# Sliding attention in one inference step: the rotary half swap on VectorE, softmax's small operations per pair of heads, and another order of pairs

## The reference, cut to what matters

```
q, k, v = split(rms_norm(x) @ w_qkv)        # 16 query heads, 4 key/value heads, 64 wide
q, k = rope(q), rope(k)                     # [x1*cos - x2*sin, x2*cos + x1*sin], halves of 32
s = q @ k^T / 8, masked by chunks of 64 (own chunk and two before)
m = max(max(s), sink); p = exp(s - m)
p = p / (sum(p) + exp(sink - m))
out = (p @ v) @ w_out
```

## Time and profile before

| | |
|---|---|
| runs, us | 1117.15, 1115.31, 1117.17 |
| profiled execution, us | 1115.43 |
| its span, us | 1113.6 |
| TensorE busy | 1103.8 us (99%) |
| VectorE busy | 703.9 us (63%) |
| ScalarE busy | 511.2 us (46%) |
| GpSimd busy | 114.1 us (10%) |
| mean granted TensorE clock | 0.995 |

### The profile page before, as it was taken

The page is one execution under the profiler, slowest core; times in us unless marked ns, Lnnn a source line. Parts: engine busy times, 40 slices in busy tenths (PEclk is TensorE's granted clock), DMA queues, the critical chain, the costliest instruction groups (busy, mean ns, idle before and its releaser), DMA issues.

```text
span 1113.6 us, 21313 instructions
## 1 busy us (share of the span) xinstructions
PE 1103.8 (99%) x8147; PEld 1080.8 (97%) x8147; DVE 703.9 (63%) x1079; ACT 511.2 (46%) x760; POOL 114.1 (10%) x146
## 2 busy tenths in 40 slices
PE   9999999999999999999999999999999999999998
PEld 8999999998999999999999999999988899999998
DVE  7766665474665876665546666655599776666442
ACT  6544443363554544444335444433466554444331
POOL 0000001200002600000210000011142410000011
PEclk9999999999999999999999999999999999999999
DMA  7544454333233644445434445543332244444431
GB/s 274 190 151 173 179 183 178 118 114 109 100 129 111 207 172 167 172 165 206 159 113 168 172 151 173 201 164 142 114 148 92 83 173 160 172 167 179 176 136 43
DMA packets 24493, 172.07 MB, mean 155 GB/s; under 512 B 3280, under 2 KB 3568, under 8 KB 5888
## 3 DMA queue, kind: packets, MB, share of 16 engines
q1 hardware_dynamic: 22320, 167.45, 42.0%
q0 software_dynamic: 960, 2.23, 0.6%
q10 hardware_dynamic: 1168, 1.77, 0.5%
HBM read 168.88 MB, written 2.56 MB: 154 GB/s over the span
## 4 chain that ended last, share of the span: by engine, by line
PE 93%; DVE 4%; ACT 1%; DMA 1%; issue 1%; POOL 0%; SPq 0%; DVEq 0%; ACTq 0%
PE acc L395 30%; PE acc L397 29%; PE acc L396 29%; DVE wlo L382 1%; DMA raw<-in_w 1%; PE num L464 1%; DVE rstd L1042 1%; PE mb L675 0%; PE mb L694 0%; PE mb L609 0%; PE num L601 0%; PE acc L722 0%; ACT work L955 0%; ACT whi L353 0%; PE mb L422 0%
## 5 line engine op out<-in xcount | busy, mean ns | idle before, releaser
L395 PE MATMUL acc<-xhi,whi 128*128 128x288 f32 x1680 | 502.2, 299 | 0.3 <-DVE wlo L382 0.3
L353 ACT ACTIVATE whi<-raw 128x1024 fp32r<-128x1024 f32 (+1 forms) x290 | 326.6, 1128 | 381.2 <-PE acc L397 363.3
L396 PE MATMUL acc<-xlo,whi 128*128 128x288 f32 x1680 | 497.0, 296 | 0.0
L397 PE MATMUL acc<-xhi,wlo 128*128 128x288 f32 x1680 | 495.3, 295 | 0.0
L382 DVE TENSOR_TENSOR wlo<-raw,whi 128x1024 fp32r<-128x1024 f32 (+1 forms) x290 | 384.2, 1326 | 158.0 <-ACT whi L353 147.3
L395 PEld LDWEIGHTS acc<-xhi,whi 128*128 128x128 f32 x1680 | 316.1, 188 | 3.0 <-issue 1.8
L397 PEld LDWEIGHTS acc<-xhi,wlo 128*128 128x128 f32 x1680 | 317.7, 189 | 0.0
L396 PEld LDWEIGHTS acc<-xlo,whi 128*128 128x128 f32 x1680 | 316.8, 189 | 0.5
L395 PE MATMUL acc<-ahi,whi 128*128 128x288 f32 x832 | 247.1, 297 | 0.9 <-DVE alo L1279 0.7
L396 PE MATMUL acc<-alo,whi 128*128 128x288 f32 x832 | 245.4, 295 | 0.0
L397 PE MATMUL acc<-ahi,wlo 128*128 128x288 f32 x832 | 244.6, 294 | 0.0
(11 more groups left out here) (225 smaller groups left out, 642.9 us busy)
## 6 DMA issues: line engine op xcount, KB each, us to landing
raw<-in_w SPq DMA_DIRECT2D x113, 1024.0 KB, 4.8
raw<-in_w SPq DMA_DIRECT2D x32, 1408.0 KB, 5.8
x<-in_xT SPq DMA_DIRECT2D x4, 288.0 KB, 5.3
raw<-in_w SPq DMA_DIRECT2D x4, 256.0 KB, 4.8
out_yT<-x ACTq DMA_DIRECT2D x2, 288.0 KB, 2.2
out_yT<-x SPq DMA_DIRECT2D x2, 288.0 KB, 2.3
work<-in_cst POOLq DMA_DIRECT2D x1, 560.0 KB, 4.2
work<-in_c ACTq DMA_DIRECT2D x1, 514.0 KB
```

Source lines behind the costliest of these rows:

```text
L353: act.activation(dst, src, ACT.Copy).then_inc(hi_done, 1)
L395: pe.matmul(out, wh, hi[:, k, :], start=(first and n == 0), stop=False)
L396: pe.matmul(out, wh, lo[:, k, :], start=False, stop=False)
L397: mm = pe.matmul(out, wl, hi[:, k, :], start=False, stop=(last and n == len(tiles) - 1))
```

## The change

- The permutation matmul goes. The channels of each q and k head are laid out in another order on the host (`ROPE_DIM`, undone for the key output), so that partners are 16 partitions apart within a block of 32. VectorE's `stream_shuffle` then swaps them while it reads the piece from PSUM, a second operation multiplies the piece by the cosine, and GpSimd multiplies the shuffled one by the sine and adds. The reciprocal of the norm and the tables are made ahead of the first evacuation. The stage has 16 groups in PSUM instead of 24.
- The negated maximum, the denominator's sum and the reciprocal are made once for the two heads of a pair. A new small sum (`s_z`) lets ScalarE make the sink's exponential once per pair. One of a pair's four scalings goes to ScalarE (`scaled`).
- The order of pieces has q1 ahead of v0. Pairs start at the pieces of `PAIR_AT`, from the third on; the sample's second pair comes before the last prompt pair. An odd tick stands between the two halves of a piece. A set of transposes comes three ticks behind its item instead of two. `FILL` holds 84 matmuls instead of 48.
- The transposed v is copied in two groups (`turn`, `last`).

```diff
-SWA_PIECES = ["k0", "q0", "v0", "q1", "q2", "q3", "k1", "q4", "q5", "q6", "v1", "q7"]
+SWA_PIECES = ["k0", "q0", "q1", "v0", "q2", "q3", "k1", "q4", "q5", "q6", "v1", "q7"]
-TURN_AFTER = {"q1": "v0", "v1": "v1"}
+TURN_AFTER = {"q2": "v0", "v1": "v1"}
-FIRST_TICK = 4
+PAIRS = [("p", 0), ("p", 1), ("p", 2), ("p", 3), ("s", 0), ("p", 4), ("p", 5), ("p", 6), ("s", 1), ("p", 7)]
+NP = len(PAIRS)
+PAIR_AT = {2: 0, 3: 1, 5: 2, 6: 3, 7: 4, 8: 5, 9: 6, 10: 7}
+TAIL_TICKS = range(2 * len(PAIR_AT), 2 * NP + 5)
+FILL = {17: [(0, [0, 1])], 18: [(0, [2, 3])], 19: [(1, [0, 1]), (1, [2, 3]), (2, [0, 1])], 20: [(2, [2, 3])],
+        21: [(3, [0, 1]), (3, [2, 3])], 23: [(0, [4, 5, 6])], 24: [(m, [4, 5, 6]) for m in (1, 2, 3)]}
...
+ROPE_DIM = np.array([16 * (l // 32) + l % 16 + 32 * (l % 32 // 16) for l in range(HD)])
+SWAP_16 = [i ^ 16 for i in range(32)]
```

TensorE (the bodies of `transposes`, `pair_scores` and `values` are those of the old tick, cut apart; `transposes` also waits for ScalarE's scaling):

```diff
             def tick(t, G0):
+                transposes(t - 3)
+                if t % 2 == 0:
+                    pair_scores(t // 2)        # waits: neg_ready of the pair before, rope_done or ks_ready
+                else:
+                    values((t - 5) // 2, G0)   # waits: pt_ready, evac of ("last", v), olo_ready
...
             def swa_in(i):
                     if what == "piece":
                         if n == 0:
                             first_two(i, c0_, G0)
                         if n > 1:
-                            in_piece(i, 0, c0_ + n, g, G0 + g)
-                    elif what == "swap":
-                        pe.wait_ge(evac, max(G0 + group_of("piece", p) + 1, G0 + g - 3))
-                        pe.matmul(bank, perm, s_raw[:, ROPE.index(p) % 2, :], start=True, stop=True).then_inc(turn_mm, 1)
+                            t = 2 * PAIR_AT[n - 1] + 1 if n - 1 in PAIR_AT else None
+                            in_piece(i, 0, c0_ + n, g, G0 + g, between=None if t is None else lambda: tick(t, G0))
+                        if n in PAIR_AT:
+                            tick(2 * PAIR_AT[n], G0)
```

ScalarE:

```diff
+                probs_turned(t - 3)
+                if t % 2 == 0:
+                    scaled(t // 2 - 1)
+                    outputs_hi((t - 6) // 2)
+                    exps(t // 2)
...
+                for n, p in enumerate(SWA_PIECES):
+                    hi_ahead(0, c0_ + n)
+                    if n in PAIR_AT:
+                        tick(2 * PAIR_AT[n])
+                        tick(2 * PAIR_AT[n] + 1)
```

VectorE and GpSimd:

```diff
                     if what == "piece":
+                        if n == 0:
+                            rms(norm + 1)
+                            dve.tensor_tensor(rc, cos, rstd[:, :], ALU.mult)
+                            dve.tensor_scalar(nsnk, sinks, -1.0, None, ALU.mult)
+                            own(dve.tensor_tensor(rs, sin, rstd[:, :], ALU.mult))
...
+                            if xi >= 2:
+                                dve.wait_ge(rope_done, xi - 1)
+                            dve.stream_shuffle(s_sw[:, xi % 2, :], bank, SWAP_16)
+                            dve.tensor_tensor(s_t1[:, xi % 2, :], bank, rc, ALU.mult).then_inc(evac, 1)
+                        if n in PAIR_AT:
+                            outputs_lo(PAIR_AT[n] - 3)
+                            scores(PAIR_AT[n])
+                        lo_ahead(0, c0_ + n)
+                        if n in PAIR_AT:
+                            divide(PAIR_AT[n])
...
+                pool.tensor_tensor(s_sw[:, b, :], s_sw[:, b, :], rs, ALU.mult).then_inc(t1_ready, 1)
                 pool.wait_ge(t1_ready, xi + 1)
+                pool.tensor_tensor(dst, s_t1[:, b, :], s_sw[:, b, :], ALU.add).then_inc(rope_done, 1)
```

More of the change, by code:

```diff
@@ L644, in mlstm_out @@
                 mix_rest(i)
-            def tick(t, G0):
[L649 to L702, removed]
-                        for u in range(2):
-                            kv = 2 * c + u
-                            pe.matmul(mb[3][u * HD:(u + 1) * HD, 0:128], s_v[0:TS, 2, kv * HD:(kv + 1) * HD],
-                                      probT[0:TS, (t - 4 + u) % 4, 128:256], start=False, stop=True, **kw).then_inc(pv_mm, 1)
@@ new lines, in transposes @@
+            def transposes(n):
+                if not 0 <= n < 2 * NP:
+                    return
+                pe.wait_ge(p_ready, n + 1)
+                if PAIRS[n // 2][0] == "p":
+                    pe.wait_ge(p_act, sum(k == "p" for k, _ in PAIRS[:n // 2 + 1]))
+                if n >= 1:
+                    pe.wait_ge(pt_ready, n)
+                pr = prob[:, n % 4, :]
+                if PAIRS[n // 2][0] == "p":
+                    for j in range(3):
+                        mm = pe.transpose(mb[2][:, j * P:(j + 1) * P], pr[:, j * P:(j + 1) * P], ident)
+                else:
+                    pe.transpose(mb[2][:, 0:P], pr[:, 0:P], ident)
+                    mm = pe.transpose(mb[2][0:TS, P:2 * P], pr[:, P:P + TS], ident)
+                mm.then_inc(pt_mm, 1)
@@ new lines, in divide @@
+            def divide(n):
+                if not 0 <= n < NP:
+                    return
+                b = n % 2
+                p = PAIRS[n][0] == "p"
+                parts = ((0, P), (P, 3 * P)) if p else ((0, CACHE + TS),)
+                J = len(parts)
+                dve.wait_ge(exp_ready, n + 1)
+                own(dve.tensor_tensor(s_den[:, b, :, 0:J], s_sum[:, b, :, 0:J], s_sk[:, b, :, 0:J], ALU.add))
+                dve.reciprocal(s_inv[:, b, :, 0:J], s_den[:, b, :, 0:J]).then_inc(inv_ready, 1)
+                dve.wait_ge(inv_ready, n + 1)
+                for u in range(2):
@@ L1308, in swa_in @@
[L1308 to L1316 removed]
+                            xi = ROPE.index(p)
                             if xi >= 2:
@@ new lines, in swa_in @@
+                        if n in PAIR_AT:
[4 more added lines that the diff above has]
+                            divide(PAIR_AT[n])
+                    else:
+                        j = int(p[1]) * P
+                        bank = acc[(g + BANK) % 4]
+                        dve.wait_ge(turn_mm, TURNS.index((what, p)) + 1)
+                        if what == "turn":
@@ L1331, in swa_in @@
-                    tick(t)
+                        outputs_lo((t - 6) // 2)
+                        scores(t // 2)
+                        divide(t // 2)
             dve.memset(zero[:, :].bitcast(F32), 0.0).then_inc(z_ready, 1)
@@ L1453, in _ @@
             pool.dma_start(a["kT_out"], s_k[:, :, TP - P:T]).then_inc(out_dma, 16)
-            pool.wait_ge(evac, G0 + group_of("turn", "v1") + 1)
+            pool.wait_ge(evac, G0 + group_of("last", "v1") + 1)
             pool.dma_start(a["v_out"][0:P, :], s_v[:, 1, :]).then_inc(out_dma, 16)
@@ L1509, in layouts @@
     first = {"q": 0, "k": KD, "v": KD + 2}
-    a["w8"] = pieces(q[:, [first[p[0]] + int(p[1]) for p in SWA_PIECES]].reshape(D, -1), 2)
+    q = q[:, [first[p[0]] + int(p[1]) for p in SWA_PIECES]]
+    for n, p in enumerate(SWA_PIECES):
+        if p in ROPE:
+            q[:, n] = q[:, n].reshape(D, 2, HD)[:, :, ROPE_DIM].reshape(D, P)
+    a["w8"] = pieces(q.reshape(D, -1), 2)
     a["w9"] = pieces(pairs(v["swa_w_out"][0], 0), 2)
```

319 lines of the change are left out of this document (165 added, 154 removed).

## The result

The changed kernel took 1131.92 us (median of four runs, 1130.77 to 1132.86), beside 1116.23 us for the kernel before on the same chip (four runs, 1114.27 to 1117.17): ratio 1.0138, 95% interval 1.0117 to 1.0158. It is slower, by 15.7 us. The forecast was 1126.8 us in a range of 1120.5 to 1132.5: the sign and the range hold, 5 us of size are missing. The range holds narrowly: the median lies 0.6 us inside its upper end.

The account below looks back on a forecast made before the run. TensorE was taken as the bound nearly everywhere. The terms, 6.9 + 1.2 + 2.9 + 3.5 + 2.5 + 2.2 - 5.9 - 2.7 = +10.6 us, led to 1126.8 us, range 1120.5 to 1132.5.

Parts of the forecast that it names:

- First scores: TensorE stall after the third piece, waiting for k0 and q0 to be rotated: 6.9 us, bounds 5.0 and 7.0.
- The clock: TensorE's granted clock dropping after the idle time before the first scores: 1.2 us lost, bounds 0 and 3.
- Small stalls: Waits for q2's rotation, for VectorE and ScalarE between pieces, and before the first late fill: together 2.9 us.
- the ring: VectorE and ScalarE operations done in turn per piece: 6.2 to 6.3 us a round, stopping TensorE a little.
- Values of pair 4: In the middle of the last piece, values wait for turned v1's copy: 3.5 us, bounds 2.7 and 4.0.
- Sample pair: Its scores, after the last piece, wait for q7's rotation: stall 2.5 us, bounds 2.3 and 3.3.
- Old waits credited: TensorE's earlier waits, mostly in the tail, removed by more fill: 2.7 us saved, bounds 0 and 2.7.
- Swaps: Ten permutation matmuls of 0.59 us each leave TensorE: 5.9 us saved, bounds 5.0 and 7.2.
- halves: Cutting 8 pieces in two around transposes and values costs TensorE 0.27 us each: 2.2 us, bounds 0 and 3.
- The beat without waits: TensorE's time per pair of heads and piece: 6.3 us before, less 0.59, plus 0.27, gives 6.0 us.
- rival (b): 0.7 us more ring stalls in six pieces and a second slow clock stretch: +6, about 1133 us; chance 0.10.

Follow-up runs that it names:

- lock1: part1 with GpSimd's sine product and add cut to the last 32 columns, sine part left out elsewhere: 1116.50 us, ratio 1.0013.
- locka: The changed kernel with GpSimd's sine product and add cut to the last 32 columns: 1127.94 us, ratio 1.0111.
- warm: The changed kernel with 44, 22 and 18 unused products of zeros in TensorE's three long waits: 1127.22 us, ratio 1.0110.
- turn: The changed kernel with VectorE copying the turned v1 before the last piece's division, not after: 1127.62 us, ratio 1.0116.
- best1: The changed kernel with seven pairs from the fifth piece on, another fill and more last projection work in three tiles: 1121.14 us, ratio 1.0058.
- best3: best2 with 24 products of zeros before the first scores: 1119.87 us, ratio 1.0040.
- part1: The kernel before with the half swap on VectorE's shuffle; also adjacent ticks and turned v copied in two groups: 1121.55 us, ratio 1.0067.
- best2: The changed kernel with pairs from the fourth piece, first evacuations before splits, earlier v1 copy, moved fill, more last projection work: 1121.19 us, ratio 1.0066.

## Why the prediction was right, and where its size was off

**First scores (6.9 us).** 6.73 measured, released by GpSimd's add, whose two first steps fell against the splits as worked out (1.71 and 1.79). Right. My upper bound of 7.0 held; the lower, 5.0 if they shared, is excluded by lock1 and locka, where a 32-column step lasts as long as the split beside it.

**The clock (1.2 us).** This is the term that failed, and by more than its upper bound of 3. warm puts it at 5.4 us of stage. I counted one dip of 1.5 us and gave the second to a rival. From the first scores to the second pair's the changed kernel needs 6.19 us (810.21 to 816.40), warm 4.25: the first dip slowed TensorE by 1.9 us. From the last piece's values to the second set of values behind them, without what lies between the transposes and the sample pair's scores, it needs 14.98 us (862.86 to 881.09), warm 10.59 (859.50 to 873.66): the second dip slowed it by 4.4. The waits of 3.48 and 3.25 us lie only 5.4 us apart, and the clock was not back between them. Together that is 6.3 us of TensorE's own work. turn, which halves the first of these waits, gets back 1.7 us beyond its waits.

**Small stalls (2.9 us).** 0.7 at q2, 0.6, 0.2 and 0.3 for ScalarE's copies in the ring, 1.1 before the late fill: 2.9. Right in sum; q2's was half of what I took, the ring's a little more.

**Values of pair 4 (3.5 us).** 3.48; turn shows the cause.

**Sample pair (2.5 us).** 3.25, the upper bound: GpSimd's add fell beside the last piece's split (1.65 instead of 0.8). I knew the mechanism and left it out of the value.

**Old waits credited (2.7 us).** They went, but a new one came that I had not looked for: 1.36 us ahead of the projection's fifth tile (896.39), which waits for VectorE's low split. FILL takes 84 matmuls out of the first four tiles, so each has only three left at the end, and the split of the fifth tile's weights has no cover. best1 to best3 give three tiles more work there, and it is gone.

**Swaps (-5.9) and halves (+2.2).** No run isolates them. With the other terms as measured, and with TensorE's whole slowing since the waits are taken as the changed kernel has them, 6.73 + 6.3 + 2.9 + 3.48 + 3.25 + 1.36 - 2.7 = 21.3, against 17.2 of the stage, they come to -4.1, where I had -3.7. The beat without waits is 5.9, predicted 6.0.

The misses are then 5.1 (clock), 0.75 (sample), 1.36 (fifth tile), -0.4 (swaps and halves) and -0.2 (first scores): together 6.6 us, the difference between +10.6 and +17.2. That the median still fell inside the range is in part luck: its value is nearer to the 1133 of rival (b), which had the second slow stretch, than to my 1126.8. The other half of that rival, 0.7 us more of ring stalls in six pieces, did not come.

**What I left out.** That a copy and a multiply on VectorE become a shuffle and a multiply is true of the counts, but says nothing of what runs beside them. part1 shows that the swap on VectorE, put into the old order, costs 6.8 us of stage instead of saving 5.9. By lock1, 4.3 of that come from GpSimd's steps, which now follow the evacuation at once and meet VectorE's scaling and split; its share of the clock is in both numbers. How much part1 loses by its two ticks side by side is not shown. The changed order hides this in the steady pieces, where GpSimd takes 0.80 and 0.81; at both ends it doesn't.

**What stays open.** What decides whether the clock falls behind the tail's short waits (best2 and best3 differ there), and whether the pairwise operations alone, with the permutation matmul kept, would gain; that kernel was not run. Why best1 to best3 still lose, between ScalarE's copies, VectorE's chain and the clock, is read from their waits and not tested one by one.

## What to carry to other kernels

An operation taken off the busiest engine is only worth its time if what replaces it doesn't sit in front of the first consumer: count the chain from the input to the first use at both ends of the stage, not only the beat. When a change makes an engine idle for several microseconds, price the clock behind it too, and look at where the next wait stands: here two waits 5.4 us apart had one slow stretch of 13.7 us around them. And if work moves to GpSimd, look at which of VectorE's SBUF operations it will stand beside.

## What the runs showed of the hardware

- A shuffle of 128x288 from PSUM is recorded with 0.48 us and takes 0.37 to the next start (803.80 to 804.17), of which loading its mask is 0.01: my 0.37. The estimate that I had worked out from the Trainium skill, "VectorE: DVE Perf Modes", the perf-mode tier table, was 0.34 us.
- The exclusion of VectorE and GpSimd also holds for small operations: a 32-column product took 1.16 instead of 0.25 us and a 32-column copy 1.29 instead of 0.21, each beside a split of 1.22. Beside VectorE's shuffle and multiply out of PSUM (808.40 to 809.23), GpSimd's step at 808.50 took its usual 0.79.
- TensorE's granted clock fell to the lower level behind waits of quite different length: 6.73 us in the changed kernel, 1.85 us in part1, and 1.17 us at the end of best3, the last of several small waits, behind which it stayed at 1.00 in best2. 84 products of zeros in the waits kept it at 1.00, worth 5.4 us; 24 of them in best2's first wait kept it at 1.00 there.
